# A decoder layer with 32 experts: weight loads issued in the order of use, and another order of work in the tail

## The reference, cut to what matters

```python
h = rmsnorm(x, g_pre_ffn) * (1.0 + scale_f) + shift_f
# hier_moe: top-1 group of 4, then top-2 of its 8 experts; 32 experts of width 256
hg = einsum('td,edf->tef', ht, w_g)
hu = einsum('td,edf->tef', ht, w_u)
act = silu(hg) * hu * combine[..., None]
y = einsum('tef,efd->td', act, w_d)
x = x + gate_f * rmsnorm(y, g_post_ffn)
```

## Time and profile before

| what | us |
|---|---|
| median of 3 runs | 798.15 |
| lowest and highest run | 796.47, 798.77 |
| the profiled execution | 795.45 |
| span of its profile | 793.6 |
| TensorE matmuls busy | 702.3 (88%) |
| VectorE busy | 411.6 (52%) |
| ScalarE busy | 287.9 (36%) |
| GpSimd busy | 120.9 (15%) |

### The profile page before, as it was taken

The page is one execution under the profiler, slowest core; times in us unless marked ns, Lnnn a source line. Parts: engine busy times, 40 slices in busy tenths (PEclk is TensorE's granted clock), DMA queues, the critical chain, the costliest instruction groups (busy, mean ns, idle before and its releaser), DMA issues.

```text
span 793.6 us, 9709 instructions
## 1 busy us (share of the span) xinstructions
PE 702.3 (88%) x3447; PEld 445.4 (56%) x3447; DVE 411.6 (52%) x876; ACT 287.9 (36%) x512; POOL 120.9 (15%) x148
## 2 busy tenths in 40 slices
PE   1899989898999999999999799989889868788974
PEld 0447747566776777777777688763333323333321
DVE  2386958998897666644312735654351211112128
ACT  5133254254447778532232225342121211111224
POOL 3064852210002112000000001010122111111000
PEclk9999999999997999999999999999989998999998
DMA  9989730411311030303355162798999999999962
GB/s 343 388 302 369 285 136 1 115 57 50 107 46 61 2 106 2 107 0 107 107 212 185 60 234 79 293 407 322 416 417 420 419 422 419 419 419 421 403 272 106
DMA packets 49724, 179.27 MB, mean 226 GB/s; under 512 B 9560, under 2 KB 13762, under 8 KB 35340
## 3 DMA queue, kind: packets, MB, share of 16 engines
q1 hardware_dynamic: 43732, 166.26, 53.7%
q0 software_dynamic: 4784, 8.19, 2.9%
q10 hardware_dynamic: 1160, 4.20, 1.4%
HBM read 174.13 MB, written 12.59 MB: 235 GB/s over the span
## 4 chain that ended last, share of the span: by engine, by line
PE 53%; DVE 17%; DMA 8%; issue 7%; ACT 4%; DVEq 0%; POOL 0%; ACTq 0%; SPq 0%; POOLq 0%; PEldq 0%
PE psA L479 9%; PE psA L481 8%; PE psA L480 8%; PE psS L883 6%; PE psA L912 6%; PE psG L883 5%; DVE mk_mem L1833 3%; DVE m L1832 3%; DMA y_dram<-sig_mem,tables 2%; DMA arena<-y_dram 1%; PE psT L870 1%; DVE arena_r L1781 1%; DMA xn_dram<-sig_mem 1%; DMA arena<-in_w_out_dram 1%; DMA kv<-xn_dram,tables 1%
## 5 line engine op out<-in xcount | busy, mean ns | idle before, releaser
L479 PE MATMUL psA<-arena_r 128*128 128x512 f32 x320 | 130.1, 406 | 4.7 <-DVE arena_r L1781 4.1
L480 PE MATMUL psA<-arena_r 128*128 128x512 f32 x320 | 125.9, 393 | 0.0
L481 PE MATMUL psA<-arena_r 128*128 128x512 f32 x320 | 125.8, 393 | 0.0
L1781 DVE TENSOR_TENSOR arena_r<-arena,arena_r 128x1024 fp32r<-128x1024 f32 (+1 forms) x37 | 60.5, 1657 | 38.5 <-ACT arena_r L1305 37.6
L479 PEld LDWEIGHTS psA<-arena_r 128*128 128x128 f32 x320 | 60.9, 190 | 25.6 <-issue 13.7
L883 PE MATMUL psS<-arena,kv 128*64 128x512 f32 x224 | 64.6, 664 | 11.1 <-issue 10.9
L481 PEld LDWEIGHTS psA<-arena_r 128*128 128x128 f32 x320 | 60.7, 190 | 13.4
L480 PEld LDWEIGHTS psA<-arena_r 128*128 128x128 f32 x320 | 61.0, 191 | 12.0 <-issue 0.2
L883 PE MATMUL psG<-arena,kv 128*64 128x512 f32 x208 | 58.2, 611 | 4.8 <-issue 4.8
L1305 ACT CAST arena_r<-arena 128x1024 fp32r<-128x1024 f32 (+1 forms) x31 | 49.8, 1629 | 20.7 <-DMA arena<-in_w_in_dram 10.1
L2278 DVE TENSOR_TENSOR sig_mem<-sig_mem,psS 128x256 f32<-128x256 f32 x8 | 4.9, 613 | 81.7 <-ACT sig_mem L1624 81.7
(11 more groups left out here) (440 smaller groups left out, 1293.2 us busy)
## 6 DMA issues: line engine op xcount, KB each, us to landing
arena<-in_w_e_gate_dram SPq DMA_DIRECT2D x25, 1024.0 KB
arena<-in_w_e_up_dram SPq DMA_DIRECT2D x25, 1024.0 KB
arena<-in_w_in_dram SPq DMA_DIRECT2D x11, 2048.0 KB, 8.3
arena<-in_w_e_down_dram SPq DMA_DIRECT2D x12, 1024.0 KB, 15.6
qs_mem<-in_w_e_down_dram SPq DMA_DIRECT2D x10, 1024.0 KB, 19.7
arena<-in_w_ada_dram SPq DMA_DIRECT2D x4, 2048.0 KB, 17.1
qT<-in_w_ada_dram SPq DMA_DIRECT2D x6, 1024.0 KB, 5.4
gvs<-in_w_ada_dram SPq DMA_DIRECT2D x5, 1024.0 KB, 6.2
```

Of the source, the lines that this page charges most:

```text
L479: nc.tensor.matmul(acc, lhs[0], rhs[0], start=start, stop=False)
L480: nc.tensor.matmul(acc, lhs[0], rhs[1], start=False, stop=False)
L481: return nc.tensor.matmul(acc, lhs[1], rhs[0], start=False, stop=stop)
L1781: V.tensor_tensor(lo[:, part], src[:, part], hi[:, part], ALU.subtract).then_inc(lo_ready, 4 if q is None else 1)
```

## The change

It does two things.

1. SP's loads: the helper `experts` is cut in two, `next_gate_up` and `next_down`, each with its own wait. Pair 2's gate and up loads go out ahead of pair 1's down loads, and for pairs 3 to 12 the gate and up loads of pair j+1 go ahead of the down loads of pair j. From pair 13 on the order is as before.
2. The tail: both halves of the last pair are copied ahead of all scaling and combining; the crowded experts' branch comes ahead of the load of the rows, which happens once; the table of the square roots is asked for ahead of the first scaling; ScalarE's and VectorE's steps are ordered anew; and tile 1 is summed on TensorE as tiles 2 and 3 are, with the last pair's part first and the combined rows second.

```diff
@@ -353,7 +353,7 @@
         fsq_in, ex_sub = sem("fsq_in"), sem("ex_sub")
         hot_ready = sem("hot_ready")
         hi_ready, lo_ready = sem("hi_ready"), sem("lo_ready")
-        fw_late, sum_ready, sum_full = sem("fw_late"), sem("sum_ready"), sem("sum_full")
+        sum_ready, sum_full = sem("sum_ready"), sem("sum_full")
         where, moe_base = {}, {}
         sum_banks = ((("T0", NPAIR), ("T1", NPAIR)), (("S1", None), ("G", NPAIR // 2)), (("O", NPAIR), ("S0", NPAIR // 2)), (("A0", NPAIR), ("A1", NPAIR)))
 
@@ -939,24 +939,34 @@
                     gate_up_product(NPAIR + v, 0, 1, OV_LOADS + v, "G", NPAIR // 2 + v)
                     turn_act(NPAIR + v, 0)
                     down_product(NPAIR + v, 0, 1, OV_LOADS + v)
-                pe.wait_ge(fss_ready, 4)
-
-            pe.wait_ge(yb_ready, NPAIR)
-            for tt in range(TT):
-                if tt >= 2:
-                    pe.wait_ge(sum_ready, (1, 3)[tt - 2])
+
+            def last_part(tt):
+
                 for half, (name, turns) in enumerate(sum_banks[tt]):
                     if name == "S1":
                         take("S1", "sum")
                     else:
-                        pe.wait_ge(bank[name].free, base[name] + turns)
-                    if tt >= 2:
-                        nc.tensor.matmul(ps[name][:, :], ident[:, :], yc[:, tt, 0, 512 * half:512 * (half + 1)], start=True, stop=False)
-                for half, (name, turns) in enumerate(sum_banks[tt]):
+                        pe.wait_ge(bank[name].free, base[name] + turns + (0 if name == "S0" else n_ov))
                     if half:
                         pe.wait_ge(yb_act, NPAIR)
-                    last = nc.tensor.matmul(ps[name][:, :], last_hot[:, tt, :], yb[:, 1, 512 * half:512 * (half + 1)], start=(tt < 2), stop=True)
+                    last = nc.tensor.matmul(ps[name][:, :], last_hot[:, tt, :], yb[:, 1, 512 * half:512 * (half + 1)], start=True, stop=(tt == 0))
+                if tt == 0:
+                    last.then_inc(sum_full, 1)
+
+            def other_part(tt):
+
+                pe.wait_ge(fss_ready, tt + 1)
+                for half, (name, _) in enumerate(sum_banks[tt]):
+                    last = nc.tensor.matmul(ps[name][:, :], ident[:, :], yc[:, tt, 0, 512 * half:512 * (half + 1)], start=False, stop=True)
                 last.then_inc(sum_full, 1)
+
+            pe.wait_ge(yb_ready, NPAIR)
+            for tt in range(3):
+                last_part(tt)
+            other_part(1)
+            last_part(3)
+            other_part(2)
+            other_part(3)
 
 
         @block.sync
@@ -1028,18 +1038,23 @@
             def down(z, q, e):
                 sp.dma_start(down_sets[z][q], wed_v[bass.ds(e, 1), :, :].rearrange("a p n -> p (a n)")).then_inc(wd_in[z], 16)
 
-            def experts(z, e0, e1_, g=None, g_turn=None, turn=None):
-
-
-                if g is not None:
-                    sp.wait_ge(bank[g].full, moe_base[g] + g_turn)
+            def next_gate_up(z, e0, e1_, g, g_turn):
+
+                sp.wait_ge(bank[g].full, moe_base[g] + g_turn)
                 gate_up(z, 0, e0)
                 gate_up(z, 1, e1_)
-                if turn is not None:
-                    sp.wait_ge(bank["A1"].full, moe_base["A1"] + turn)
+
+            def next_down(z, e0, e1_, turn):
+
+                sp.wait_ge(bank["A1"].full, moe_base["A1"] + turn)
                 down(z, 0, e0)
                 down(z, 1, e1_)
 
+            def pair_gate_up(j):
+                next_gate_up(j % 3, 2 * j, 2 * j + 1, MOE_G[(j - 3) % 2], (j - 3) // 2 + 1)
+
+            def pair_down(j):
+                next_down(j % 3, 2 * j, 2 * j + 1, j - 2)
 
             first_gate_up(0)
             sp.wait_ge(ring_out, item_at[("proj", 1)] + 1)
@@ -1051,17 +1066,22 @@
             gate_up(1, 0, 2)
             gate_up(1, 1, 3)
             sp.wait_ge(ring_out, len(items))
+            gate_up(2, 0, 4)
+            gate_up(2, 1, 5)
             down(1, 0, 2)
             down(1, 1, 3)
-            gate_up(2, 0, 4)
-            gate_up(2, 1, 5)
             sp.wait_ge(x1_ready, 2 * TT)
             sp.wait_ge(xss_ready, TT)
             down(2, 0, 4)
             down(2, 1, 5)
-            for j in range(3, NPAIR - 1):
-
-                experts(j % 3, 2 * j, 2 * j + 1, MOE_G[(j - 3) % 2], (j - 3) // 2 + 1, j - 2)
+            pair_gate_up(3)
+            for j in range(3, OWN_DOWN):
+                pair_gate_up(j + 1)
+                pair_down(j)
+            pair_down(OWN_DOWN)
+            for j in range(OWN_DOWN + 1, NPAIR - 1):
+                pair_gate_up(j)
+                pair_down(j)
             j, z = NPAIR - 1, (NPAIR - 1) % 3
             sp.wait_ge(bank[MOE_G[(j - 3) % 2]].full, moe_base[MOE_G[(j - 3) % 2]] + (j - 3) // 2 + 1)
             for half in range(2):
@@ -1074,27 +1094,18 @@
                 down(z, q, 2 * j + q)
             y_v = y_dram.rearrange("(w t p) n -> t p w n", w=2, p=P)
 
-            def y_load():
-
-                for tt in range(TT):
-                    sp.dma_start(yc[:, tt, :, :], y_v[tt]).then_inc(yc_in[tt], 16)
-
-            for b in range(2):
-                sp.wait_ge(y_stored[b], 16 * (NPAIR // 2))
-            y_load()
             sp.wait_ge(slot_ready, 2)
             n_ov = sp.value_load(ovi[0:1, NOV:NOV + 1], min_val=0, max_val=NOV // 2)
             with sp.If(n_ov > 0):
-                sp.wait_ge(fss_ready, 2)
-                for tt in (2, 3):
-                    sp.wait_ge(yc_in[tt], 16)
                 with sp.Fori(0, n_ov) as v:
                     e_a = sp.value_load(ovi[0:1, bass.ds(2 * v, 1)], min_val=0, max_val=NE - 1)
                     e_b = sp.value_load(ovi[0:1, bass.ds(2 * v + 1, 1)], min_val=0, max_val=NE - 1)
-                    experts(1, e_a, e_b, "G", NPAIR // 2 + v, NPAIR + v)
-                sp.wait_ge(y_stored[0], 16 * (NPAIR // 2 + n_ov))
-                y_load()
-
+                    next_gate_up(1, e_a, e_b, "G", NPAIR // 2 + v)
+                    next_down(1, e_a, e_b, NPAIR + v)
+            sp.wait_ge(y_stored[1], 16 * (NPAIR // 2))
+            sp.wait_ge(y_stored[0], 16 * (NPAIR // 2 + n_ov))
+            for tt in range(TT):
+                sp.dma_start(yc[:, tt, :, :], y_v[tt]).then_inc(yc_in[tt], 16)
             for tt in range(TT - 1):
                 sp.wait_ge(fin_ready, tt + 1)
                 sp.dma_start(out_v[:, tt, :], x1(tt)).then_inc(out_done, 16)
@@ -1661,14 +1672,6 @@
                     act_taken(j - 1, (j - 1) % 2)
                 if j >= OWN_DOWN:
                     act_taken(j, j % 2)
-
-            def first_choice(tt, loads, done):
-
-                act.wait_ge(yc_in[tt], 16 * loads)
-                nc.scalar.activation(yc[:, tt, 0, :], yc[:, tt, 0, :], ACT.Copy, scale=rt[:, 9, tt:tt + 1]).then_inc(done, 1)
-
-            first_choice(0, 1, fw_ready)
-            first_choice(1, 1, fw_ready)
             y_right(NPAIR - 1, 1, NPAIR // 2)
             with act.If(n_ov > 0):
                 with act.Fori(0, n_ov) as v:
@@ -1676,26 +1679,39 @@
                     gate_silu(NPAIR + v, 0, "G", NPAIR // 2 + v)
                     act_taken(NPAIR + v, 0)
                     y_right(NPAIR + v, 0, NPAIR // 2 + v)
-                first_choice(0, 2, fw_ready)
-                first_choice(1, 2, fw_ready)
-                for tt in (2, 3):
-                    act.wait_ge(yc_in[tt], 32)
-            first_choice(2, 1, fw_late)
-            first_choice(3, 1, fw_late)
             scratch2 = stage_mem[:, 0:D]
 
-            nc.scalar.activation(st[:, 44:45], st[:, 34:35], ACT.Sqrt)
-            for tt in range(TT):
-                if tt < 2:
-                    act.wait_ge(sum_ready, (2, 4)[tt])
+            def first_choice(tt):
+
+                act.wait_ge(yc_in[tt], 16)
+                nc.scalar.activation(yc[:, tt, 0, :], yc[:, tt, 0, :], ACT.Copy, scale=rt[:, 9, tt:tt + 1]).then_inc(fw_ready, 1)
+
+            def square(tt):
+
+                if tt == 0:
+                    act.wait_ge(sum_ready, 1)
                     nc.scalar.activation(scratch2, yc[:, tt, 0, :], ACT.Square, accum_out=st[:, tt:tt + 1]).then_inc(fms_ready, 1)
-                else:
-                    act.wait_ge(sum_full, tt + 1)
-                    for half, (name, _) in enumerate(sum_banks[tt]):
-                        n = tt + 20 * half
-                        nc.scalar.activation(scratch2[:, 512 * half:512 * (half + 1)], ps[name][:, :], ACT.Square, accum_out=st[:, n:n + 1]).then_inc(fms_ready, 1)
+                    return
+                act.wait_ge(sum_full, tt + 1)
+                for half, (name, _) in enumerate(sum_banks[tt]):
+                    n = tt + 20 * half
+                    nc.scalar.activation(scratch2[:, 512 * half:512 * (half + 1)], ps[name][:, :], ACT.Square, accum_out=st[:, n:n + 1]).then_inc(fms_ready, 1)
+
+            def rooted(tt):
+
                 act.wait_ge(fsq_in, tt + 1)
```

(55 more changed lines are left out.)

## The result

The changed kernel takes **791.62 us** in the median of 20 runs (787.6 to 797.51), the one before 797.51 us in 20 runs: ratio 0.9929, 95% interval 0.9914 to 0.9944, which is 5.7 us less (4.5 to 6.9). The forecast was 791.85 and 6.3 us less. The profiled execution took 791.58 us, its span 789.5.

What follows compares the result with a forecast made beforehand. The prediction took the rate of weight transfers to bound the expert stage and VectorE the end. Stage 4.3 plus tail 2.0 us made 6.3, off the 798.15 us median: 791.85 us (chance 0.52), range 787.9 to 796.3.

Steps and rivals of the forecast that it cites:

- The hole: Weight transfers between 545 and 555 us, ahead of the plateau, run below 420 GB/s; filling this gives 3.9 us.
- by 751: Sign of being wrong: the last gate and up weights land later than 751 us.
- The order: Expert stage: pair 13's gate and up weights come two loads, 5.7 us, earlier; with later waits the stage gives 4.3 us.
- That isn't the gain: Pair 13 beginning at 712.4 us isn't the gain: all weights together come only 3.9 us earlier, and pair 14 meets them.
- the wait for pair 14: TensorE, ready for pair 14 at 731.2 us, waits 3.4 us for weights; its product then takes 8.78 us.
- rival (a): Expert stage gives its most: pair 14's wait under 3 us, product not slowed, 7.7 us in all, 790.4 us; chance 0.25.
- the down products wait for their weights: Sign of being wrong in the expert stage; down weights were counted as covered by over 8 us.
- the bound of 5.7 us: Stage's upper bound: pair 14's product runs fast and the second half of pair 15's weights decides, 5.7 us.
- The tail: From the last expert pair to the end, VectorE's one list sets the time; 2.0 us come out, bounds 0.6 and 3.3.
- rival (c): Tail: the switch of tables costs 2.7 us of exposed time, not 1.3; total 4.9 us, 793.2 us; chance 0.07.
- (b): Expert stage: the hole only moves and the stage gives nothing, the tail its 2.0 us; 796.2 us; chance 0.11.
- (d): Plateau, 549 to 750 us: the longer backlog lowers the transfer rate; at 395 GB/s 12 us slower, 803.9 us; chance 0.05.

Runs made afterwards that it cites:

- one swap: Kernel before with only pair 4's gate and up loads moved ahead of pair 3's down loads, old tail: 0.9959; with the new tail: 0.9921.
- all but the swap: Kernel before with the new load order from pair 5's gate and up loads on, pair 3's down loads still ahead of pair 4's, old tail: 0.9984.
- the one kept busy: Changed kernel with the roots' table asked for behind tile 2's scaling, plus ten TensorE matmuls whose sum is not read: 0.9925 against the kernel before.

## Why the prediction was right

**The hole.** I took 3.9 us, the whole of it. In the changed kernel 0.8 us are left, by the windows above, so 3.1 came; with one swap 3.5. The last gate and up load landed at 735.97 + 18.38 = 754.35, 212.0 us behind pair 1's begin, where it was 215.4: 3.4 us. The place and the cause were right, shown by the swap alone and by all but the swap; the size was 0.4 to 0.8 us too large. By this the load landed, on the time axis of before, at 751.5 and not by 751, which the prediction had named as a sign of being wrong. It was a sign of that half microsecond, and of no more.

**The order.** "That isn't the gain" was the step that mattered, and it held: pair 13 began 8.5 us earlier (9.6 forecast), pair 14 6.0, the last down product 4.55. The forecast named the wait for pair 14 (3.4 us; 2.72 and 4.31 measured) and a product of 8.78 (7.1 and 9.58). A product of 8.78 came in none of the six profiles with the new order. Its 4.3 us of stage lie between the two executions, 4.55 and 2.89. That the sum came out between two outcomes, neither of which was the one it describes, is luck; the wait itself was foreseen. Forecast and rival (a) were not two cases, as I had put them, but two outcomes of one kernel. Six profiles with the new order give 2.9 to 5.7 us, 4.0 in the mean; three with the single swap 3.0 to 3.9, 3.5. The half microsecond between them is not shown to be there.

**A wait that was not in the sum.** The prediction said that it is wrong if the down products wait for their weights, and gave no term to those of pair 15. Before, their second load was issued at 740.58 and landed 19.6 us later, at 760.2, and the product began at 762.25: 2.0 us to spare. After, it landed 218.1 us behind pair 1's begin, 2.6 us earlier than before and not 3.9, while TensorE would have been ready 5.0 us earlier. So the product waited, 0.89 us instead of 0.46. Of the bound of 5.7 us the last gate and up load left 5.0 (pair 15's product ended that much earlier), and the down weights took 0.4 more: 4.55. In three more profiles the pause is 0.88 to 0.94 us; the landing stands in none of them, so there it is inferred from the like pause.

**The tail.** 2.0 forecast, 2.00 and 1.99 measured, by the steps named: table load exposed, list without a gap of over 0.3 us, 3.10 us from tile to tile (777.91, 781.01, 784.12 above). The list began 0.3 us later than forecast and took 0.4 us less up to tile 1's root (9.57 us where 9.95 had been added up), so that two small errors cancel. The price of the table was put at 1.28 us; with the root that asks for it, it was 1.36, so rival (c) falls. By the Trainium skill, "ScalarE: Activation LUTs", section "What ACT_TABLE_LOAD costs", a switch costs about 2.66 us with its drain. The trace doesn't agree for this place: moving the load out of the way gave 1.36.

**What I had no term for.** The last down product, for most of its length at half clock: 5.2 to 5.4 us in three of nine profiles with the new tail (the one kept busy not counted), in none of the four with the old one. All three lie among the four profiles with the pause of 0.9 us ahead of it, and with the pause of 0.46 it never came, so that the pause goes with it rather than the tail. The old tail hung on the landing of the third tile and would probably have hidden it, which no profile shows; the new one hangs on this product, so that it costs its 1.6 to 1.7 us. It may be why the runs give 5.7 where stage and tail of the first profile give 6.55, as may the long wait for pair 14, or plain spread; the runs without a profile can't be asked.

**Rivals.** (b), the hole only moves, falls with the run that has one swap. (d), a lower rate, falls with the plateau's 416 to 420 GB/s. The crowded experts' branch was not entered, as forecast.

## What to carry to other kernels

Where transfers set a stage, look for the idle time ahead of their plateau and for the wait in the issuing queue that makes it; reordering loads inside the plateau moved the waits here to where the lead was spent, and no gain from it could be told. Follow the last load of every kind to its landing: the one with 2 us to spare before becomes the bound once the rest is 4 us faster. Ask of every operation that a tail begins with what had hidden it before: here a table load of 1.3 us came onto the path, and it had a pause two steps later. A product behind an idle stretch may run at half clock in one execution and not in the next, so one profile doesn't price a stage whose end hangs on such a product.

## What was not expected of the hardware

Pair 1's gate product began between 538.07 and 544.33 us in fourteen profiles, though the code ahead of it is the same but for the order of a few loads; a spread of 6.3 us, where the runs of the kernel before spread over 7.5. In the earliest TensorE had spent 17 us at the lower clock until then, in the latest 38 us; between them the two don't always go together (24 us and 541.44, 27 us and 539.47), so the clock is a part of it at most. TensorE's clock fell at the last down product (0.68 and 0.75 in the windows above) in three of the four executions with a pause of 0.9 us ahead of it; in the fourth, the first profile of the changed kernel, it stayed at 1.00 behind a pause of 0.89. Late in the stage, with many loads outstanding, SP's issue of a load took 2.1 us and more, where it takes 0.43 otherwise. That isn't the time of a load, as the line of 2.13 us is one of 512 KB, which are 1.25 us at 420 GB/s. Whether it delays what stands behind it in SP's program was not tested.
